# A Hymba-style layer in fp32 on one core: x transposed unnormalised, its factor applied where banks are emptied

## What is computed

```python
h  = concat([meta, x])                                  # (1040, 2048)
hn = h * rsqrt(mean(h * h, -1) + EPS) * norm_g
pv, pg, q, k, v, ag = split(hn @ w_in[layer])
pool_out = multiscale_pool(pv)         # mean over 2, 4, 8, 16 frames minus the frame, a linear map per group, a scale
attn_out = attention(rmsnorm(q), rmsnorm(k), v)         # chunks of 64, window 128, meta keys, a sink per head
mixed = concat([silu(pg) * pool_out, silu(ag) * attn_out])
out = (h + mixed @ w_out)[16:]
```

## Time and profile before

| | |
|---|---|
| runs | 1261.69, 1263.39 and 1263.98 us, median 1263.39 |
| profiled execution | 1263.45 us, span of the instructions 1261.8 us |
| TensorE busy | 1239.5 us, 98% of the span |
| VectorE, ScalarE, GpSimd busy | 896.2 (71%), 635.4 (50%), 68.6 us (5%) |
| granted TensorE clock | 0.999 of full speed |
| DMA | 134.38 MB, mean 106 GB/s |

### The profile page before, as it was taken

How to read it: one execution, slowest core, us unless ns; L and a number is a source line. 1 busy time by engine, 2 the same in 40 slices (tenths; PEclk the granted TensorE clock), 3 DMA queues, 4 the chain that set the end, 5 groups by cost and what they waited for, 6 DMA issues and landing times.

```text
span 1261.8 us, 19307 instructions
## 1 busy us (share of the span) xinstructions
PE 1239.5 (98%) x6200; PEld 1042.5 (83%) x6200; DVE 896.2 (71%) x1425; ACT 635.4 (50%) x1490; POOL 68.6 (5%) x78
## 2 busy tenths in 40 slices
PE   4999999999999999999999999999999999999998
PEld 4988898898988987888888888888888888788887
DVE  6557786888879886665644677788798887854553
ACT  6434456465563654544533344655646556444442
POOL 0000000010010110000000000000101103000000
PEclk9999999999999999999999999999999999999999
DMA  5232333222332225544533333222322222343442
GB/s 211 83 92 78 96 96 85 84 77 67 101 92 78 73 67 206 188 137 147 189 126 91 91 94 88 83 82 86 98 72 88 75 92 88 112 133 125 166 142 84
DMA packets 70609, 134.38 MB, mean 106 GB/s; under 512 B 8064, under 2 KB 10240, under 8 KB 69888
## 3 DMA queue, kind: packets, MB, share of 16 engines
q1 hardware_dynamic: 68160, 125.17, 31.6%
q0 software_dynamic: 2384, 8.39, 1.9%
HBM read 125.14 MB, written 8.39 MB: 106 GB/s over the span
## 4 chain that ended last, share of the span: by engine, by line
PE 94%; DVE 3%; DMA 1%; ACT 1%; issue 1%; SPq 0%; ACTq 0%
PE R L1059 19%; PE R L1060 18%; PE R L1063 18%; PE S L1282 4%; PE S L1283 4%; PE S L1281 4%; PE OP L1283 2%; PE OP L1281 2%; PE R L1282 2%; PE OP L1282 2%; PE R L1283 2%; PE R L1281 2%; PE OP L1060 1%; PE OP L1063 1%; PE OP L1059 1%; PE OP L1207 1%
## 5 line engine op out<-in xcount | busy, mean ns | idle before, releaser
L430 ACT ACTIVATE wh<-raw 128x512 fp32r<-128x512 f32 x400 | 250.4, 631 | 494.4 <-PE R L1063 269.8
L725 DVE TENSOR_TENSOR wl<-raw,wh 128x512 fp32r<-128x512 f32 x400 | 282.1, 708 | 241.7 <-ACT wh L430 240.5
L1059 PE MATMUL R<-act_h,wh 128*128 128x512 f32 (+1 forms) x1168 | 426.2, 370 | 0.0
L1060 PE MATMUL R<-act_l,wh 128*128 128x512 f32 (+1 forms) x1168 | 422.5, 367 | 0.0
L1063 PE MATMUL R<-act_h,wl 128*128 128x512 f32 (+1 forms) x1168 | 403.2, 365 | 0.0
L1059 PEld LDWEIGHTS R<-act_h,wh 128*128 128x128 f32 x1168 | 220.1, 188 | 36.9 <-DVE wl L725 0.8
L1060 PEld LDWEIGHTS R<-act_l,wh 128*128 128x128 f32 x1168 | 220.0, 188 | 34.7
L1063 PEld LDWEIGHTS R<-act_h,wl 128*128 128x128 f32 x1168 | 210.5, 188 | 36.8
L949 DVE RECIPROCAL scr<-scr 128x512 f32<-128x512 f32 x32 | 107.3, 3353 | 1.1
L402 POOL TENSOR_TENSOR scr<-scr 128x527 f32<-128x527 f32 (+3 forms) x40 | 50.6, 1265 | 799.2 <-ACT pv_last L430 364.4
L430 ACT ACTIVATE pm<-OP 16x128 fp32r<-16x128 f32 x256 | 68.3, 267 | 5.4
(11 more groups left out here) (206 smaller groups left out, 1825.0 us busy)
## 6 DMA issues: line engine op xcount, KB each, us to landing
raw<-w_in_blocks SPq DMA_DIRECT2D x272, 256.0 KB, 2.6
raw<-w_out_in SPq DMA_DIRECT2D x128, 256.0 KB, 3.0
scr<-xcat SPq DMA_DIRECT2D x32, 256.0 KB, 4.3
mixed<-xcat SPq DMA_DIRECT2D x4, 1024.0 KB, 8.3
res<-xcat SPq DMA_DIRECT2D x16, 256.0 KB, 3.2
out<-scr POOLq DMA_DIRECT2D x14, 256.0 KB, 2.6
out<-res POOLq DMA_DIRECT2D x14, 256.0 KB, 4.9
scr<-pool_w_in SPq DMA_DIRECT2D x8, 256.0 KB, 3.2
```

Of the source, the lines that this page charges most:

```text
L430: return nc.scalar.activation(dst, src, ACT.Copy)
L725: return nc.vector.tensor_tensor(dst, a, b, ALU.subtract)
L1059: mm(o, wh[:, b, w], act_h[:, k, c], start=(k == 0), stop=False)
L1060: mm(o, wh[:, b, w], act_l[:, k, c], start=False, stop=False)
```

## The change

1. **Start.** x is transposed as loaded. It comes in five loads by columns (k 0-1, 2-3, 4-7, 8-11, 12-15, each for all 512 frames), with weight blocks between them; the identity comes ahead of the other constants. TensorE first does five products of zeros (kT, just cleared) into R[0], which are overwritten. K and V blocks alternate; the transposes go with the K blocks only.
2. **The factor of each frame** (first half; the second half is still normalised ahead of its transposes) is computed from x later: the squares behind the last splits of the K and V blocks, a broadcast, five transposes after the first query block (r_transposes) and a copy to rb, the factors as a row on every partition. VectorE multiplies by rb whenever it empties a bank (scaled); in the second half it multiplies by 1.0 instead.
3. **Banks** are emptied by VectorE throughout: kv_out in step 1 of the queries, q_out, gate_in, pv_out. Queries are squared from mixed. K's squares, sums and root, in the V tile before, stand in steps 2 to 4 of the queries, its inversion in step 4 (k_norm, VectorE, 512 or 528 columns). In the queries, square_low moves from step 4t + 4 to 4t + 5 (behind the split), sum_squares a block later, q_sqrt from 4t + 5 to 4t + 6, q_norm from 4t + 6 to 4t + 7. The V transposes (v_windows) move from block 0 to block 8.
4. **Gates**: 0.5 * x * (1 + tanh(x/2)) with gate_in (VectorE), gate_tanh (ScalarE) and gate_out (VectorE, one operation); the 0.5 is in o_out and in the pooling scale.

The diff, cut to its core:

```diff
+WARM = 5
...
-FIRST_SPLITS = {2: 2, 5: 3, 7: 4, 11: 5, 15: 6}
+FIRST_SPLITS = {0: (0,), 3: (1, 2), 7: (3, 4), 11: (5, 6), 15: (7,)}
+FIRST_LOADS = ((0, 2), (2, 4), (4, 8), (8, 12), (12, 16))
...
+        QB = [S[:, 0, :]] + [(R[1][:, :], R[0][:, :], O)[t % 3] for t in range(PAIRS - 1)]
...
+            def first_frames(i):
+                k0, k1 = FIRST_LOADS[i]
+                lo, hi = k0 % 4 * P, (k1 - 1) % 4 * P + P
+                sp.dma_start(mixed[:, k0 // 4:KT:4, lo:hi],
+                             xcat[META:META + HALF, k0 * P:k1 * P].rearrange("(r p) c -> p r c", p=P)).then_inc(s_xf[i], 16)
+            def first_block(n, free=True):
+                load_block(n, n % RAW, w_in[TILE_BLKS * (n % 2) + n // 2, :, :], free)
+            sp.dma_start(cst[:, 0:P], consts[:, 0:P]).then_inc(s_id, 16)
+            sp.dma_start(x_meta, xcat[0:META, :]).then_inc(s_xmeta, 16)
+            first_frames(0)
+            sp.dma_start(vec[:, :], vecs).then_inc(s_vec, 16)
+            first_block(0, free=False)
+            first_frames(1)
+            first_block(1, free=False)
+            first_frames(2)
+            first_block(2, free=False)
+            first_block(3, free=False)
+            first_frames(3)
+            sp.dma_start(cst[:, P:C_N], consts[:, P:C_N]).then_inc(s_cst, 16)
+            first_frames(4)
             for h in range(HALVES):
                 h0 = h * NBLK
                 for n in range(RAW if h == 0 else 0, KV_BLKS):
-                    load_block(h0 + n, n % RAW, w_in[n, :, :])
+                    load_block(h0 + n, n % RAW, w_in[TILE_BLKS * (n % 2) + n // 2, :, :])
...
+            act.wait_ge(s_vec, 16)
+            act.wait_ge(s_xg, 1)
+            copy(act_h[:, :, 0:META], meta_g).then_inc(s_xh, 1)
+            def first_stats(r):
+                stats(x_first[r], P, r, r, r)
             for k in range(KT):
...
+                for off in FIRST_SPLITS.get(k, ()):
+                    split_high(0, off)
+            act.wait_ge(s_cst, 16)
...
+            first_stats(0)
+            first_stats(1)
+            act.wait_ge(s_init, 5)
...
-                for s in range(4 if h == 0 else 0, 5):
+                for s in range(5 if h == 0 else 0, KV_BLKS):
                     split_high(h4, s + LEAD)
-                product_done(act, h, 0)
-                for bank, c in span_banks(h, KB[h]):
+                    if h == 0 and s < 7:
+                        first_stats(s - 3)
+                if h == 0:
+                    act.wait_ge(s_xm, 1)
+                    root(META, ROWT)
+                def r_columns():
+                    act.wait_ge(s_xrs, 2)
+                    for r in range(ROWT):
+                        copy(r_col[:, r, :], xrs[:, r:r + 1].to_broadcast([P, P])).then_inc(s_rc, 1)
+                    copy(r_meta, xrs[0:META, ROWT:ROWT + 1].to_broadcast([META, P])).then_inc(s_rc, 1)
+                def r_rows():
+                    act.wait_ge(s_rt, 1)
+                    copy(rb[:, META:COLS], PT[:, :]).then_inc(s_rb, 1)
+                    copy(rb[:, 0:META], PM[:, 0:META]).then_inc(s_rb, 1)
...
                 def q_square(t):
-                    product_done(act, h, KV_BLKS + t * TILE_BLKS)
+                    act.wait_ge(s_qv, h * PAIRS + t + 1)
                     if t >= 2:
                         act.wait_ge(s_qss, h * PAIRS + t - 1)
                     for dst in (q_sq[t % 2], q_sqh[t % 2]):
-                        nc.scalar.activation(dst, QB[t % 4][:, :], ACT.Square).then_inc(s_qsq, 1)
+                        nc.scalar.activation(dst, mixed[:, PAIRS + t, :], ACT.Square).then_inc(s_qsq, 1)
                 def q_sqrt(t):
                     act.wait_ge(s_qss, h * PAIRS + t + 1)
-                    act.wait_ge(s_qn, QB_FREE + h * PAIRS + max(t - 1, 0))
+                    if t >= 2:
+                        act.wait_ge(s_qn, h * PAIRS + t - 1)
                     nc.scalar.activation(q_rs[t % 2], (PT, PM)[t % 2][:, :], ACT.Sqrt,
                                          scale=1.0 / HD, bias=eps).then_inc(s_qsd, 1)
                 for s in range(Q_BLKS + 1):
...
+                    if s == 1 and h == 0:
+                        r_rows()
+                    if s == 2:
+                        k_square()
+                    if s == 4:
+                        k_sqrt()
                     if s and s % 4 == 0:
                         q_square(s // 4 - 1)
-                    if s < Q_BLKS:
-                        split_high(h4 + KV_BLKS // RAW, s + LEAD)
-                    if s > 4 and s % 4 == 1:
+                    if s > 4 and s % 4 == 2:
                         q_sqrt(s // 4 - 1)
-                    if s == 2:
+                    if s == 10:
                         v_all_out()
                     if s == 18:
...
+                    def gate_tanh(n):
+                        act.wait_ge(s_gv[n], ONE + G + 1)
+                        if n:
+                            act.wait_ge(s_gt[n - 1], ONE + G + 1)
                         else:
...
+                            act.wait_ge(s_gt[3], ONE + G)
+                        nc.scalar.activation(gate_t, gate[n], ACT.Tanh, scale=0.5).then_inc(s_ge[n], 1)
...
-                        if s == 12:
-                            pv_out(0)
-                        elif s == 16:
-                            pv_out(1)
                         if s < G_BLKS:
...
+                def scaled(dst, src, c):
+                    if h == 0:
+                        return nc.vector.tensor_tensor(dst, src, rb[:, c], ALU.mult)
+                    return nc.vector.tensor_scalar(dst, src, 1.0, None, ALU.mult)
+                def kv_out():
+                    dve.wait_ge(s_rb, 2)
+                    dve.wait_ge(s_blk, ONE + h * NBLK + KV_BLKS - 1)
+                    for bank, c in span_banks(h, KB[h]):
+                        scaled(k_own[:, c], bank, c).then_inc(s_ke, 1)
...
+                def q_out(t):
+                    product_done(dve, h, KV_BLKS + t * TILE_BLKS)
+                    scaled(mixed[:, PAIRS + t, :], QB[t], slice(META, COLS)).then_inc(s_qv, 1)
                 def q_norm(t):
                     n = h * PAIRS + t
                     dve.wait_ge(s_qsd, n + 1)
                     nc.vector.reciprocal(q_rs[t % 2], q_rs[t % 2]).then_inc(s_qrs, 1)
                     dve.wait_ge(s_qrs, n + 1)
-                    nc.vector.scalar_tensor_tensor(mixed[:, PAIRS + t, :], QB[t % 4][:, :], gq8[:, :],
+                    nc.vector.scalar_tensor_tensor(mixed[:, PAIRS + t, :], mixed[:, PAIRS + t, :], gq8[:, :],
                                                    q_rs[t % 2], ALU.mult, ALU.mult).then_inc(s_qn, 1)
                 for s in range(Q_BLKS + 1):
                     if s and s % 4 == 0:
-                        square_low(s // 4 - 1)
+                        q_out(s // 4 - 1)
                     if s < Q_BLKS:
                         split_low(h4 + KV_BLKS // RAW, s + LEAD)
-                    if s > 4 and s % 4 == 2:
+                    if s == 1:
+                        kv_out()
+                    if s == 2:
+                        k_square_low()
+                    if s == 4:
+                        k_norm()
+                    if s > 4 and s % 4 == 1:
+                        square_low(s // 4 - 1)
+                    if s > 4 and s % 4 == 3:
...
+                square_low(PAIRS - 1)
...
-                    def silu(n, bank):
+                        nc.vector.scalar_tensor_tensor(mixed[:, bass.ds(PAIRS + g * 2 + u // 2, 1), cols],
+                                                       o_sum.unsqueeze(1), 0.5, gate[u // 2][:, cols].unsqueeze(1),
+                                                       ALU.mult, ALU.mult).then_inc(s_oe, 1)
+                    def gate_in(n, bank):
+                        product_done(dve, h, n0 + (0, 4, 16, 20)[n])
+                        scaled(gate[n], bank[:, :], slice(META, COLS)).then_inc(s_gv[n], 1)
+                    def gate_out(n):
                         dve.wait_ge(s_ge[n], G + 1)
...
+                        nc.vector.scalar_tensor_tensor(gate[n], gate_t, 1.0, gate[n],
+                                                       ALU.add, ALU.mult).then_inc(s_gt[n], 1)
+                    def pv_out(jj):
+                        product_done(dve, h, n0 + 8 + 4 * jj)
+                        for bank, c in span_banks(h, PVB[h][jj]):
+                            scaled(pv[jj][:, c], bank, c)
+                        last = pv_last[:, bass.ds(g * 2 + jj, 1), :]
+                        if h == 0:
+                            ins = nc.vector.tensor_tensor(last, bank[:, SUB - META:SUB].unsqueeze(1),
+                                                          rb[:, COLS - META:COLS].unsqueeze(1), ALU.mult)
+                        else:
+                            ins = nc.vector.tensor_scalar(pv[jj][:, 0:META].unsqueeze(1), last, 1.0, None, ALU.mult)
+                        ins.then_inc(s_pve, 1)
...
```

(61 more changed lines are left out.)

279 lines of the change are left out of this document (113 added, 166 removed).

## The result

| | before, same chip | after | ratio |
|---|---|---|---|
| median of 4 runs | 1263.05 us (1261.69 to 1263.98) | 1319.99 us (1317.00 to 1323.34) | 1.0452 [1.0438, 1.0467] |
| profiled execution | 1263.45, span 1261.8 | 1317.00, span 1315.0 | |

The change makes the kernel 57 us slower; the forecast said 31 slower, and 1303 at most.

The account below looks back on a forecast made before the run. The prediction took TensorE, busy 1239.5 of 1261.8 us, as the bound. Its terms -12.7 + 2.9 + 18.4 + 23.2 - 0.9 = +30.9 on 1263.45 gave 1294 us, range 1283 to 1303 for the forecast alone, 1271 with two rivals.

Parts of the forecast that it names:

- What bounds: Whole kernel: TensorE is busy 1239.5 of 1261.8 us, unbroken from 19.09; any new wait there costs its full length.
- Part 1: Start: without normalisation ahead of the transposes, the query stage starts earlier; minus 12.7 us (minus 10.5 to minus 14).
- Part 2: After the first query block: TensorE waits for the frame factors, finished late; plus 2.9 us (2 to 4).
- Part 3: Query stage: VectorE's queue delays the low half of the squares, so TensorE stalls; plus 18.4 us (12 to 22).
- Part 4: Four groups of each half: pooling values leave their bank late, behind VectorE's queue; plus 23.2 us (17 to 25).
- The gate product: Gate groups: one more VectorE product queued ahead of emptying the pooling bank; 0.67 us each.
- Part 5: Two starts of the output projection: TensorE's wait for attention outputs, held up by a gate's reciprocal, goes; minus 0.9 us.
- (a): Query stage and groups: VectorE, relieved of work, runs ahead and empties banks in time; faster, 1252.7 us, chance 0.11.
- (b): Only the gate groups stall, as the query chain fits; 1275 us, chance 0.08.
- (c): Only the query stage stalls; 1271 us, chance 0.04.
- (d): Gates: tanh and exp need different ScalarE tables, two loads of 1.28 us for each of 32 gates; 1330 us, chance 0.04.
- (e): Start: it brings nothing because loads of 1 KB rows lag, and the factor is late; 1300 us or more, chance 0.03.

## Why the prediction went wrong where it did

The direction and the mechanisms hold: the parts that the forecast had come to +36.6 (-11.3 + 2.5 + 21.0 + 21.8 + 2.6), against its +30.9. What failed is the sum: **it has no term for TensorE's clock behind a wait (10.7 us), and none for the pitch of untouched products (5.5)**; with them it is +52.8 of the 53.2 measured in the profiled spans. The median is another 3 us above the profiled run, whose clock was the highest of the four (0.990 against 0.984 to 0.988). The range was made of the bounds of the terms that it had, and ended at 1303. One sign that it named failed with it: TensorE's busy time did not stay near 1240, it rose to 1265.7.

- **What bounds.** "Any new wait there costs its full length" was the failing step: in this kernel a wait of 2.3 to 3 us can cost 1.4 to 2.5 more. The rows of before could have hinted at it: behind the idle 5.38 us eight transposes took 1.97 us, where four took 0.60 later. The prediction used that for the start alone. The Trainium skill (TensorE: Matmul & The Clock Gate, HAM oscillation) describes such a failure, a TensorE that falls back to the slow clock while it waits for its next operands and starts the next piece slow. The runs here agree for some of the waits (granted clock 0.50 behind six of them in after), and the prediction did not draw on it.
- **Part 1**, -12.7: came as -11.3 (12.3 less the same 1.0), inside the part's bounds. Part of it is chance: in the profiles of the two experiments that leave before's start alone, the query stage starts at 51.33 and 51.48, not at 52.83. The first product came at 11.31, not 10.4, for the zeros and transposes ahead of it: the zeros ended at 6.2, where the forecast had 5.7 at most and said that nothing waits for them. They delay the first product by 0.7 and still save 0.2 to 0.9 by the query stage.
- **Part 2**, +2.9: 2.5, and a slow stretch of 1.4 behind it.
- **Part 3**, +18.4: 21.0 and 1.8 for the first products behind. Four of the five tiles at 1.0 us were right (0.99 to 1.18), the eighth right (2.67 against 2.7), the second mostly free, as said. Missed: in the fifth tile of each half the wait is 2.4 instead of 1.0. The rows of after show where the 1.4 come from:

  ```profile
  103.18 0.67 ACT L459 ACTIVATE band_h<-kT 64x576 fp32r<-64x576 f32 x1
  ...
  107.52 0.69 DVE L755 TENSOR_TENSOR wl<-raw,wh 128x512 fp32r<-128x512 f32 x1 [5.10 <-ACT wh L459]
  ...
  115.81 0.74 DVE L755 TENSOR_TENSOR band_x<-kT,band_h 64x576 fp32r<-64x576 f32 x1
  ```

  From 103.18 to 106.8 ScalarE copies K's band (step 18) ahead of a split. VectorE sits idle 5.10 us for it, and the inversion behind that split starts at 108.13, 14.1 us after the one before instead of 12.7. VectorE's own part of the band (115.81) comes behind the low half and delays nothing here. Not every tile of a repeating pattern has the same queue.
- **Part 4**, +23.2: 21.8, and 0.1 for each first product. The forecast's 2.9 and 3.0 came as 2.4 and 3.0. "The gate product" counts 0.6, as the kernel before with the copy alone shows.
- **Part 5**, -0.9: did not come in sum. The gates' wait is gone, but in the last group of each half, some 6 us ahead of the projection, there is a new wait of 0.5 for the probabilities (PE OP L1292, 1.0 in two). Why it is new was not followed.
- **The sums.** As printed, the terms of Part 3 add up to 17.8, not 18.4 (twice 5.0 and 2.8, with 1.3 and 0.9), and those of Part 4 to 23.6, not 23.2; both parts at their low bounds give 1282, not 1283. None of this decides anything.
- **VectorE's speed.** The row of 692 ns was taken, and after's rows bear it out: VectorE empties 512 columns in 0.69 and 0.68, where ScalarE took 0.60. The Trainium skill (ScalarE: Activation LUTs, Rules for kernel authors) advises VectorE for multiplications, with a factor of up to about three over ScalarE, which it gives for bf16. For fp32 from a bank nothing of it shows here.
- **Rivals.** (a) fell: the pooling copy starts 2.4 and 2.9 us behind its tile's end in the two places shown, where 0.5 was the bound. (b) and (c) fell, since both places stall. (d) fell: after has six table loads, as before, the groups of ScalarE's rows being

```profile
L459 ACT ACT_TABLE_LOAD x4 | 5.1, 1283 | 0.1
L490 ACT ACT_TABLE_LOAD x1 | 1.3, 1283 | 0.9 <-PEq L1442 0.9
L478 ACT ACT_TABLE_LOAD x1 | 1.3, 1283 | 0.0
```

  so going from exp to tanh loads nothing. (e) fell: the start brought its 12.3.

The chances of the sign were sound; the range was not, since it varied only terms that were in the sum.

## What to carry to other kernels

Where TensorE hardly rests, put nothing that frees its banks behind work that can wait: an operation moved to a less busy engine is late by that engine's queue, not by its load. Book a wait of more than 2 us on TensorE as its length and a risk of 1.4 to 2.5 us more, as it was here, and widen the range by it. When products that nobody changed take longer at full clock, compare where their operands lie, and put new small tiles behind the large ones.

## What the runs showed of the hardware beyond what was expected

- Behind waits of 2.2 to 2.9 us TensorE's granted clock was 0.50 for some microseconds in six places of after's run and 1.00 in others of the same length: products at 0.43 us instead of 0.23, 1.4 to 2.5 us lost each time. The mean clock varies from run to run (0.984 to 0.990), and the time with it (1323 to 1317 us). Behind waits of up to 1.1 us in the groups no such stretch was seen.
- The pitch of a product of 512 columns in the projection was 229.7 ns or 233.3, by the position of the tiles alone; 96 unused bytes cost before 5.9 us. Which address property decides, and whether it is the moving operand, the weights or both, was not settled.
- Five products of zeros ahead of the first transposes made the first products fast (0.13 to 0.15 us apart instead of 0.22) and started them 0.7 us later; by the query stage they had saved 0.2 to 0.9 us.
